# Expert weights in 640 half transfers of 512 KB, spread over the TensorE's code blocks

## What is computed

```
def moe_swiglu(h, router_w, w_gate, w_up, w_down):
    xt = h.reshape(B * T, D)
    logits = (xt @ router_w).astype(jnp.float32)
    top_val, top_idx = lax.top_k(logits, TOP_K)
    gates = jax.nn.softmax(top_val, axis=-1)
    combine = jnp.einsum("nk,nke->ne", gates, jax.nn.one_hot(top_idx, N_EXPERTS, dtype=jnp.float32))
    y = jnp.zeros((B * T, D), dtype=jnp.float32)
    for e in range(N_EXPERTS):
        y = y + combine[:, e:e + 1] * swiglu(xt, w_gate[e], w_up[e], w_down[e]).astype(jnp.float32)
    return y.reshape(B, T, D).astype(h.dtype)
```

## Time and profile before

| | |
|---|---|
| median of three runs | 1587.73 us (1581.73 to 1588.0) |
| profiled execution, and its span | 1578.8 us, 1577.0 us |
| PE busy | 1450.5 us, 92% of the span |
| VectorE, ScalarE, GpSimd busy | 16%, 11%, 9% |
| bytes moved by DMA | 433.47 MB |
| expert stage | from about 632 to 1562 us |

### The profile page before, as it was taken

One profiled execution on the slowest core, in us unless ns is written; L12 is line 12 of the kernel. 1 busy time (PEld: TensorE's weight loads), 2 busy tenths in 40 slices (PEclk: granted clock), 3 DMA queues, 4 the chain that ended last, 5 costly groups with the idle time before them and its releaser, 6 DMA issues.

```text
span 1577.0 us, 54544 instructions
## 1 busy us (share of the span) xinstructions
PE 1450.5 (92%) x25973; PEld 1260.1 (80%) x25973; DVE 254.1 (16%) x490; ACT 177.1 (11%) x383; POOL 143.1 (9%) x167
## 2 busy tenths in 40 slices
PE   9999999999999999888888898998998898988887
PEld 8786587777687865888888888888888788988886
DVE  3433310000143435000010010010010010000102
ACT  4123220000131332100000000000000000000001
POOL 2243200000022532200000000000000000000000
PEclk9999999999999999999999999999999999999999
DMA  9213344444242245999999999999999999999992
GB/s 341 98 43 134 107 161 160 160 160 148 95 160 107 68 153 225 364 382 376 362 375 362 371 373 370 379 379 372 376 371 381 349 384 369 380 358 382 385 366 110
DMA packets 133612, 433.47 MB, mean 275 GB/s; under 512 B 9082, under 2 KB 33916, under 8 KB 119052
## 3 DMA queue, kind: packets, MB, share of 16 engines
q1 hardware_dynamic: 132384, 427.69, 72.1%
q0 software_dynamic: 672, 2.14, 0.5%
q10 hardware_dynamic: 332, 0.13, 0.0%
HBM read 428.89 MB, written 1.05 MB: 273 GB/s over the span
## 4 chain that ended last, share of the span: by engine, by line
PE 89%; issue 7%; DVE 2%; ACT 1%; POOL 1%; DMA 0%; ACTq 0%; DVEq 0%
PE ps L1135 33%; PE ps L1159 16%; PE ps L984 9%; PE ps L683 8%; PE ps L995 4%; PE ps L846 4%; PE ps L694 3%; PE ps L1192 2%; PE ps L803 1%; PE ps L1064 1%; PE ps L716 1%; PE ps L813 1%; PE ps L679 1%; PE ps L709 1%; PE ps L823 1%
## 5 line engine op out<-in xcount | busy, mean ns | idle before, releaser
L1159 PE MATMUL ps<-LT_sb,ring 128*64 128x80 f32 x5376 | 202.6, 233 | 31.6 <-issue 31.0
L1159 PEld LDWEIGHTS ps<-LT_sb,ring 128*64 128x64 f32 x5376 | 195.5, 137 | 38.2 <-issue 36.3
L1135 PE MATMUL ps<-AT_sb,ring 128*64 128x80 f32 x5376 | 200.4, 233 | 26.4 <-issue 26.2
L1135 PE MATMUL ps<-wpost,ring 128*64 128x80 f32 x5376 | 200.4, 233 | 22.7 <-issue 21.1
L1135 PEld LDWEIGHTS ps<-AT_sb,ring 128*64 128x64 f32 x5376 | 194.6, 138 | 31.7 <-issue 31.0
L1135 PEld LDWEIGHTS ps<-wpost,ring 128*64 128x64 f32 x5376 | 193.8, 139 | 28.5 <-issue 25.9
L984 PEld LDWEIGHTS ps<-hT_sb,ring 128*128 128x128 f32 x768 | 136.2, 191 | 24.4 <-issue 9.1
L984 PE MATMUL ps<-hT_sb,ring 128*128 128x256 f32 (+1 forms) x768 | 155.7, 362 | 0.0
L683 PE MATMUL ps<-hT_sb,ring 128*128 128x256 f32 x576 | 128.2, 380 | 0.0
L683 PEld LDWEIGHTS ps<-hT_sb,ring 128*128 128x128 f32 x576 | 108.3, 190 | 14.8 <-DVE late L1637 0.5
L1988 POOL TENSOR_SCALAR small<-small 128x1 f32<-128x1 f32 x16 | 3.6, 222 | 1191.6 <-ACT late L1515 923.1
(11 more groups left out here) (285 smaller groups left out, 1148.8 us busy)
## 6 DMA issues: line engine op xcount, KB each, us to landing
ring<-in_moe_w_gate SPq DMA_DIRECT2D x84, 1024.0 KB, 8.5
ring<-in_moe_w_up SPq DMA_DIRECT2D x84, 1024.0 KB, 8.4
ring<-in_moe_w_down SPq DMA_DIRECT2D x84, 1024.0 KB, 8.0
late<-in_moe_w_up SPq DMA_DIRECT2D x28, 1024.0 KB, 8.0
late<-in_moe_w_gate SPq DMA_DIRECT2D x28, 1024.0 KB, 7.8
late<-in_moe_w_down SPq DMA_DIRECT2D x28, 1024.0 KB, 8.1
ring<-in_ffn_w_gate SPq DMA_DIRECT2D x11, 1024.0 KB, 5.4
ring<-in_ffn_w_up SPq DMA_DIRECT2D x11, 1024.0 KB, 8.1
```

The lines of the kernel that those rows point to most:

```text
L1135: ins = mm(o[lo:lo + P // 2, :], pairs[:, m % 2, lo:lo + P // 2], xgT[e % 2][:, k, :], start=(k == 0 and m % 4 == 0), stop=(k == KD - 1), ...
L1159: ins = mm(o[lo:lo + P // 2, :], d[:, i, m * P + lo:m * P + lo + P // 2], moe_hid[:, 2 * j + i, :], start=(first and m % 4 == 0), stop=las ...
```

## The change

Every unit now goes as two transfers of 512 KB, one for each half of what each partition receives: one of its two 4 KB rows (gate and up units), two of its four 2 KB rows (the chunk of 4 tiles), or one of its two 4 KB rows (down units, whose 8 KB run is thereby cut in two). Each of the 640 timed halves has a mark of its own in `HALF_TURN`, by the same rule with half the step. Each half adds 16 to the place's semaphore, so PE waits for multiples of 32. The instructions of PE, VectorE, ScalarE and GpSimd and their order stay as they are, and so do the 174 marks.

With the new numbers 134 marks let out four halves, 33 let out three, 2 let out two (marks 1 and 14) and one lets out one (134 x 4 + 33 x 3 + 2 x 2 + 1 = 640). Of the 320 second halves 286 have the mark that their unit had and 34 come one mark later; of the first halves 40 come one mark earlier.

```diff
--- before.py
+++ after.py
@@ -156,12 +156,12 @@
                     turns.add((owner, name, i))
     last = used_at[ROUND_UNITS - 1] - TURNS_AHEAD
     issues = ROUND_UNITS - N_UNIT
-    unit_turn = [max(free_at[i], 1 + i * (last - 1) // (issues - 1)) for i in range(issues)]
-    assert all(unit_turn[i] <= used_at[N_UNIT + i] - TURNS_AHEAD for i in range(issues))
-    return turns, unit_turn
-
-
-PAGE_TURNS, UNIT_TURN = page_turns()
+    half_turn = [max(free_at[h // 2], 1 + h * (last - 1) // (2 * issues - 1)) for h in range(2 * issues)]
+    assert all(turn <= used_at[N_UNIT + h // 2] - TURNS_AHEAD for h, turn in enumerate(half_turn))
+    return turns, half_turn
+
+
+PAGE_TURNS, HALF_TURN = page_turns()
 assert ROUND_UNITS % N_UNIT == 0
 N_STEPS = 25
 FIRST_STEPS = (1, 0, 2)
@@ -587,20 +587,24 @@
                         first_free(n)
                     elif first:
                         sp_.wait_ge(unit_used, n - N_UNIT + 1)
-                        sp_.wait_ge(page_turn, UNIT_TURN[n - N_UNIT])
                     else:
                         sp_.wait_ge(unit_used, per_round(r, n - N_UNIT + 1, ROUND_UNITS))
                     if kind == "d":
                         lo = (MOE_AT[c] + 2 * j) * P
-                        dst = unit_of(n)
-                        src = moe_down[0, e][lo:lo + 2 * P, :].rearrange("(p i) d -> p (i d)", p=P)
+                        dst = down_unit(n)
+                        src = moe_down[0, e][lo:lo + 2 * P, :].rearrange("(p i) d -> p i d", p=P)
                     else:
                         f = slice(MOE_AT[c] * P, (MOE_AT[c] + MOE_TILES[c]) * P)
                         ks = gate_ks(c, j)
                         dst = gate_unit(n, c)
                         src = (moe_gate if kind == "g" else moe_up)[0, e][ks.start * P:ks.stop * P, f]\
                             .rearrange("(k p) f -> p k f", p=P)
-                    sp_.dma_start(dst, src).then_inc(unit_landed[n % N_UNIT], 16)
+                    rows = dst.shape[1] // 2
+                    for hf in range(2):
+                        if first and n >= N_UNIT:
+                            sp_.wait_ge(page_turn, HALF_TURN[2 * (n - N_UNIT) + hf])
+                        sp_.dma_start(dst[:, hf * rows:(hf + 1) * rows, :], src[:, hf * rows:(hf + 1) * rows, :])\
+                            .then_inc(unit_landed[n % N_UNIT], 16)
 
             moe_loads(0, True)
             sp_.wait_ge(rounds_ready, 1)
@@ -1107,7 +1111,7 @@
                 ins.then_inc(ohT_ps, 1)
 
             def landed(r, n):
-                pe.wait_ge(unit_landed[n % N_UNIT], per_round(r, 16 * (n // N_UNIT + 1), 16 * ROUND_UNITS // N_UNIT))
+                pe.wait_ge(unit_landed[n % N_UNIT], per_round(r, 32 * (n // N_UNIT + 1), 32 * ROUND_UNITS // N_UNIT))
 
             def units_of(c, part):
 
```

## The result

The change made the kernel slower by about 7 us. Its median is 1592.58 us (1586.18 to 1601.25, 18 runs) against 1586.91 us for the kernel before (18 runs beside them); the medians lie 5.7 us apart and the means 7.1, and the ratio is 1.0045 with a 95% interval of 1.0024 to 1.0065. That of the change lies inside the 0.5% that I had called no difference, but its interval excludes 1, and its sign is not that of the forecast. The profiled execution took 1587.09 us, its span 1585.2.

The account below looks back on a forecast made before the run. The prediction took the DMA engines to set the expert stage's pace, with late code idling PE. Its terms, -17 + 4 + 6 + 3 = -4 us from the median 1587.7, gave 1583.5 us; own range 1576 to 1591, 8 in 10 within 1567 to 1602.

Parts of the forecast that it names:

- What bounds the kernel: Expert stage, 905 us: it goes at the DMA engines' speed, as queued weights delay PE's code; PE idles 99 us.
- -17 us for the thin marks: Expert stage, 17 blocks behind marks letting out one unit: filling the DMA engines there gives back 17 us.
- +4 us for the marks with three halves: Expert stage, 33 marks letting out 0.5 MB less: some blocks run dry, costing 4 us, between nothing and 13.
- +3 us for completions: All DMA engines: 320 more transfers' completions at 10 ns each cost 3 us, at most 30.
- straight line through two packet sizes: Completion price: a line through 326 ns for 8 KB and 168 ns for 4 KB meets zero bytes at 10 ns.
- +6 us for the down units' packets: 112 down units: 8 KB packets become twice as many of 4 KB, 299.6 against 293.6 us; range nothing to 14.
- The sum: Whole kernel: -17 + 4 + 6 + 3 = -4 us, from the median 1587.7 to 1583.7, said as 1583.5 us.
- The transfers themselves cost: Rival, DMA engines: each added completion costs 95 ns, 30 us in place of 3, giving 1611 us; chance 0.15.
- The fit that the prediction took from that page: Transfer estimate, 2.0 us plus bytes by 436 GB/s: 3.2 us for a half, 2,000 us for 640 in a row.
- More comes back: Rival, expert stage: all blocks at 387 GB/s give 870 us and a time of 1562, half way 1573; chance 0.17.
- The hole only spreads: Rival, 33 marks with three halves: each leaves 0.4 us, 13 us in place of 4, giving 1593 us; chance 0.16.
- What moves without a price: SP's four issues behind a mark, PE's wait for 32 and the three marks of lead: hidden, at no cost.

Follow-up runs that it names:

- the two pairs of executions: The kernel before and the changed kernel, each profiled once and then once more unchanged; the second executions took 1593.79 and 1594.87 us.
- The streams with PE: Separate test kernel: 128-matmul blocks each let out 2 MB of down weights, whole or in halves of either layout; 17-block windows took 94 to 103 us.
- the streams alone: Separate test kernel without computation: SP streams down and gate units whole or in halves; down units reached 419 GB/s whole, 404 and 403 in halves.

## Why the prediction was wrong

- *What bounds the kernel* was right. The stage goes at the speed of the DMA engines: with PE's program the same, 20 us more of q1 less the idle and overlapped time make the stage's +7 us, and PE's "issue" follows.
- *-17 us for the thin marks* was about right: the 17 blocks lose 0.7 us in place of 14.7. *+4 us for the marks with three halves* was low: their blocks went from 2.8 to 10.2 us by the share, 7 more. But other blocks lose less too, so the net over all blocks is about -13 us, as forecast. In idle time of the engines it is 9.3 and 13.6 us for the two pairs of executions. In time it is less: taking the spreading away costs 0.47%, some 7 us.
- *+3 us for completions* was right: 2.9 us, 320 x 9 ns. The straight line through two packet sizes had given 10.
- *+6 us for the down units' packets* is the step that failed. It read "two windows with full engines price that: 400 GB/s with 8 KB alone, 392 with 4 KB alone", and the window with 4 KB alone held units of the up matrix. It priced the size of a packet, and left out that a half of a down unit no longer is a stretch of memory in one piece, but every second 4 KB of one. Measured: +17.8 us by the mean packet (16.7 for all of q1 but the completions). For halves that are in one piece the same step would have held, at +6.9 with the change's marks. The other bound of that step, 382 GB/s and 14 us, was also too low.
- *The sum* with that one term replaced is -13 + 18 + 3 = +8 us, against 0.0045 x 1587 = 7 us measured (4 to 10).
- *The rivals.* "The transfers themselves cost" had the sign, but not the cause: halves in one piece at the old marks, with the same 640 transfers, are not slower than whole units (0.9986). The Trainium skill ("DMA: Bandwidth & Descriptors", section Rules for kernel authors) asks for 1 MiB or more in one transfer; for transfers that overlap, the runs bear that out by little at 512 KB: 400 against 407 GB/s for gate units alone, and nothing that shows in the kernel. The fit that the prediction took from that page is given there for transfers that GpSimd issues; these are SyncE's. "More comes back" did not come: the stage's rate fell to 369 GB/s. "The hole only spreads" named 1593 us, which is the time that came, but by luck: it is right that the 33 marks cost more than 4 us, yet they cost 7 and not 13, and the loss over all blocks fell by 13 and not by 4; what came on top was the packets.
- *What moves without a price* held: issues, lead and landings covered themselves.

Open is why the pattern slows packets beside PE's work and not alone, and why it does so almost only where the first unit of two meets the second; the middle of a group of four, where the second unit meets the third, shows nothing (170 to 174 ns in the three runs). Lying in pieces is not enough: a gate or up half takes 4 KB out of every row of 3584 floats, 14 KB, and its packets stay at 169 to 173 ns beside the same work. The streams with PE differ from those alone in PE's matmuls, in its code packets and in the pace of the issues at once, and these were not taken apart. The same page of the Trainium skill (section Latency and other measured facts) lists copies that slow down where the partitions' rows lie at large powers of two apart, 512 KiB to 8 MiB, and advises a few KiB of padding or laying tiles out in one piece; the rows here lie 8 KB apart, so it is no more than a hint, though the advice is what helped.

## What to carry to other kernels

When a transfer is cut, look at which addresses each piece takes. Here it paid to cut so that each piece stays one stretch of memory, and to change the order of the partitions for it. Price a packet by rows of the same address pattern and over a long stretch, since the median packet may not change at all while its tail does. Where the DMA engines set the pace, add up their busy time and their idle time apart; a gain in the one hid the loss in the other here.

## What the runs showed of the hardware

- Beside PE's work, a transfer that takes 4 KB out of every 8 KB needs 2.76 to 2.82 us of the 16 engines per MB, one in a single piece 2.61 to 2.67, and 8 KB runs 2.60 to 2.61. Alone, the first two are equal (404 and 403 GB/s), and 8 KB runs reach 419.
- The slower packets are a tail: the median stays 159 ns, and the share that lasts 30 ns longer goes from 4% to 9%. They sit where the first of two units meets the second (189 ns there, 171 elsewhere).
- A completion takes an engine 9 ns (2.9 us for 320 more on each).
- In this kernel 672 transfers of 512 KB cost no measurable time against 336 of 1 MB when each is one piece (0.9986, 0.9967 to 1.0006, with 883.9 us of q1 against 884.3 for whole units of the same layout). In the streams alone gate units lost 407 to 400 GB/s.
